# Gate and up products of two feed-forward blocks: token slices of 432, 424 and 424 instead of 256, 512 and 512

## The reference

```python
def swiglu(h, w_gate, w_up, w_down):
    return (jax.nn.silu(h @ w_gate) * (h @ w_up)) @ w_down

x = x + 0.5 * swiglu(rmsnorm(x, norm_ffn1[l]), w_ffn1_gate[l], w_ffn1_up[l], w_ffn1_down[l])
x = x + hybrid_mixer(rmsnorm(x, norm_mix[l]), w_in[l], ...)
x = x + 0.5 * swiglu(rmsnorm(x, norm_ffn2[l]), w_ffn2_gate[l], w_ffn2_up[l], w_ffn2_down[l])
```

## Time and profile before

| | |
|---|---|
| median of three runs | 2524.55 us |
| the profiled execution's own time | 2521.63 us |
| its span, first to last instruction | 2519.8 us |
| mean granted TensorE clock | 0.985 |
| TensorE matmul busy | 2437.7 us, 97% of the span |
| VectorE, ScalarE, GpSimd busy | 37%, 22%, 21% |

### The profile page before, as it was taken

How to read it: one execution, slowest core, us unless ns; L and a number is a source line. 1 busy time by engine, 2 the same in 40 slices (tenths; PEclk the granted TensorE clock), 3 DMA queues, 4 the chain that set the end, 5 groups by cost and what they waited for, 6 DMA issues and landing times. The chain is left out here.

```text
span 2519.8 us, 29661 instructions
## 1 busy us (share of the span) xinstructions
PE 2437.7 (97%) x12762; PEld 2037.1 (81%) x12762; DVE 923.0 (37%) x1453; ACT 555.3 (22%) x988; POOL 524.0 (21%) x283
## 2 busy tenths in 40 slices
PE   6999999999999999799998999999999999999998
PEld 5888888888888887666677878888888888888887
DVE  5322222132212246765636755622132212221224
ACT  4111111111111135533433221311111111111112
POOL 3121111111111123422213322111111111112111
PEclk8999999999999999899999999999999999999999
DMA  4110111111111125413234562011111111111012
GB/s 152 34 59 26 42 34 50 34 34 42 42 34 38 38 73 139 152 57 118 82 115 126 173 263 99 26 34 59 34 34 42 42 34 41 35 42 50 26 34 84
DMA packets 152003, 168.62 MB, mean 67 GB/s; under 512 B 15680, under 2 KB 124224, under 8 KB 151872
## 3 DMA queue, kind: packets, MB, share of 16 engines
q1 hardware_dynamic: 141504, 145.75, 18.7%
q10 hardware_dynamic: 10368, 20.98, 2.2%
HBM read 126.72 MB, written 36.70 MB: 65 GB/s over the span
## 5 line engine op out<-in xcount | busy, mean ns | idle before, releaser
L1320 PE MATMUL ps<-h_hi,w_hi 128*128 128x512 f32 (+2 forms) x2568 | 926.0, 361 | 14.4 <-ACT q_rot L806 5.8
L1321 PE MATMUL ps<-h_lo,w_hi 128*128 128x512 f32 (+2 forms) x2568 | 916.8, 357 | 0.0
L1322 PE MATMUL ps<-h_hi,w_lo 128*128 128x512 f32 (+2 forms) x2568 | 915.5, 356 | 0.0
L596 POOL TENSOR_TENSOR w_lo<-w_raw,w_hi 128x1024 fp32r<-128x1024 f32 x159 | 383.4, 2419 | 1773.6 <-ACT w_hi L721 1773.6
L1320 PEld LDWEIGHTS ps<-h_hi,w_hi 128*128 128x128 f32 (+1 forms) x2568 | 489.5, 191 | 105.5 <-issue 22.2
L1322 PEld LDWEIGHTS ps<-h_hi,w_lo 128*128 128x128 f32 (+1 forms) x2568 | 489.4, 191 | 70.5
L1321 PEld LDWEIGHTS ps<-h_lo,w_hi 128*128 128x128 f32 (+1 forms) x2568 | 490.0, 191 | 67.4
L1070 DVE TENSOR_TENSOR prod<-silu,ps 128x256 f32<-128x256 f32 x132 | 79.1, 599 | 983.0 <-PE ps L1322 978.1
L1360 PE MATMUL ps<-w_hi,hid_hi 128*128 128x512 f32 x880 | 343.0, 390 | 0.0
L1362 PE MATMUL ps<-w_hi,hid_lo 128*128 128x512 f32 x880 | 342.4, 389 | 0.0
L1361 PE MATMUL ps<-w_lo,hid_hi 128*128 128x512 f32 x880 | 342.3, 389 | 0.0
(11 more groups left out here) (131 smaller groups left out, 1495.6 us busy)
## 6 DMA issues: line engine op xcount, KB each, us to landing
w_raw<-in_w_ffn_gate SPq DMA_DIRECT2D x44, 512.0 KB, 3.8
w_raw<-in_w_ffn_up SPq DMA_DIRECT2D x44, 512.0 KB, 3.8
w_raw<-in_w_ffn_down SPq DMA_DIRECT2D x44, 512.0 KB, 3.5
w_raw<-in_w_in SPq DMA_DIRECT2D x14, 512.0 KB, 5.0
proj<-stage ACTq DMA_DIRECT2D x24, 256.0 KB, 2.1
x_mid<-x SPq DMA_DIRECT2D x10, 512.0 KB, 2.6
x<-in_x_sample SPq DMA_DIRECT2D x8, 512.0 KB, 8.2
proj<-gla_t ACTq DMA_DIRECT2D x4, 640.0 KB, 3.0
```

Of the source, the lines that this page charges most:

```text
L596: nc.gpsimd.tensor_tensor(w_lo[slot][:, :, :], w_raw[raw][:, :, :], w_hi[slot][:, :, :].bitcast(F32), ALU.subtract).then_inc(w_lo_ready, 1)
L1320: mm(out, hi, rhs_hi, start=first, stop=False)
L1321: mm(out, hi, rhs_lo, start=False, stop=False)
L1322: return mm(out, lo, rhs_hi, start=False, stop=last)
```

## The change

The old slices are kept for the first group of the first block. In all other groups (21 of 22) the slices are tokens 0 to 431, 432 to 855 and 856 to 1279. `prod` is computed with these widths, and the waits follow: for normalised tokens, the slice's end is rounded up to a whole tile; `ffn_down` waits for a slice's `hid_lo` at the tile in which the slice begins.

```diff
-SLICES = ((0, 256), (256, 512), (768, 512))
+FIRST_SLICES = ((0, 256), (256, 512), (768, 512))
+EVEN_SLICES = ((0, 432), (432, 424), (856, 424))
...
+def slices(early):
+    return FIRST_SLICES if early else EVEN_SLICES
...
# hidden on ScalarE, hidden on VectorE, and gate_up:
-                c0, n = SLICES[c]
+                c0, n = slices(A is A1 and i == 0)[c]
...
# gate_up
-                    pe.wait_ge(NORMS[n]["lo"], 2 * (c0 + m) // P)
+                    pe.wait_ge(NORMS[n]["lo"], 2 * ((c0 + m + P - 1) // P))
...
# ffn_down
-                for c, (c0, m) in enumerate(SLICES):
-                    if t * P == c0:
+                for c, (c0, m) in enumerate(slices(A is A1 and i == 0)):
+                    if t * P <= c0 < (t + 1) * P:
                         pe.wait_ge(A["hid_lo"], 6 * i + NCH + c + 1)
```

More of the change, by code:

```diff
@@ L1334, in gate_up @@
                 s = 6 * i + 3 * t + c
-                c0, m = SLICES[c]
+                c0, m = slices(A is A1 and i == 0)[c]
                 if s < NCH:
-                    pe.wait_ge(NORMS[n]["lo"], 2 * (c0 + m) // P)
+                    pe.wait_ge(NORMS[n]["lo"], 2 * ((c0 + m + P - 1) // P))
                 if c == 0:
```

## The result

The changed kernel takes 2530.34 us (median of 8 runs, 2527.72 to 2536.5) against 2524.23 us before (8 runs): ratio 1.0031, 95% interval 1.0021 to 1.0041. That is 5.3 to 10.3 us slower; the two medians differ by 6.1 us. In a second measurement (e3) the ratio was 1.0037 (1.0023 to 1.0050). The prediction was 2523.5 us and "the same"; the measured time lies inside the range, but the kernel is slower beyond the interval, so the likeliest case was wrong.

A forecast was written before the change was run, and what follows sets the result against it. TensorE's own matmul stream was taken as the bound. Matmuls 0, step between widths -0.8, ScalarE and VectorE -0.2, waits 0 gave -1.0 us: 2523.5 us on the median, "the same" (0.78), range 2517 to 2531.

The forecast's parts named there:

- What bounds the kernel: In the feed-forward groups TensorE waits for nothing; their length is the number of matmuls by the pitch of each.
- The matmuls of the changed slices: Gate and up of 21 groups: three pitches sum to 573.3 ns before and after, difference 0; bounds -80 and +215 us.
- The step between widths: The 0.02 us behind each 256-wide slice, 42 times in changed groups, was taken as gone: -0.8 us, bounds 0 and -1.7.
- ScalarE and VectorE: Their work follows the columns; only the narrower last slice at the first block's end counts: -0.2 us, bounds 0 and -0.3.
- the waits: Weight splits, raw-buffer loads, `prod` and `ffn_down` waits stay covered, with split slack falling from 6.1 to about 4.4 us: 0.
- the start of the second block: Slice 0 starts at the same place, the transposes about 3.5 us later, and later tiles stay hidden: 0.
- The misaligned third slice: Rival: rounded or misaligned columns, third slice starting at column 856 off 64 bytes, make the kernel slower; chance 0.10.
- the line: The pitch formula for a matmul of n columns at full clock: n/2.4 + 13.3 ns.
- half a block: A smaller case of the misaligned rival: half a block extra in the third slice alone, 6.7 us.
- Blocks of 16 columns: Case of the misaligned rival: TensorE handles whole blocks of 16, slices 1 and 2 cost 432 columns each: 13.4 us, 2537 us.
- The load-bound narrow slice: Rival: weight loads bind the 256-wide slice, the price per column is 0.443 ns: -13.4 us, 2511 us; chance 0.06.

The follow-up runs named there:

- e3: The changed kernel run again with no edit, against the kernel before: 2530.92 us, ratio 1.0037 (1.0023 to 1.0050).
- e2: The changed kernel with slices of 384, 448 and 448 columns, against the kernel before: 2551.29 us, ratio 1.0112 (1.0098 to 1.0127).
- e14: The changed kernel's width table set to (w, 512, 768 - w), w from 256 to 480: 512 columns cost 226.7 to 234.4 ns by start.
- e13: The changed kernel's table set to 21 triples around 300, 468, 512 and other orders: 468 columns cost 206.7 or 211.7 ns by start.
- e9: The 21 triples of a first width sweep, with 64 of 128 weight columns loaded in ten groups: 420-column slice 9.28 us before, 8.96 after.
- e7: The changed kernel's table set to other orders of widths, such as (448, 384, 448): 448 columns at token 0 cost 202.5 or 206.7 ns.

## Why the prediction was wrong, point by point

**What bounds the kernel: right.** TensorE's stream does, with no wait; this also holds after.

**The matmuls of the changed slices: the step that failed.** "The fixed part is equal at 256 and at 512, and I take it as equal between them." It is not equal between them: 15.9, 10.0 and 16.7 ns in the three new slices, and from 8.3 ns (268 columns at 0) to 22.4 (488 at 0) in the sweeps. The two widths of the trace happened to be multiples of 128 at starts that are multiples of 128, a family for which 13.3 ns held everywhere (120.0, 173.3, 226.7 ns). Two points on a line, both from a special family, said nothing of the widths between; my bounds (-80 and +215 us) admitted this, but the chance of 0.78 didn't. The term was forecast at 0 and is about +5.2 us: the three fixed parts are 42.6 ns together against 40.0, 2.6 ns x 2016. Gate and up of a group lasted 55.33 against 55.08 us, which says the same. The time stayed inside the range because the range made room for up to 3.5 ns a triple; the mechanism that was forecast, equal pitches for equal columns, is not what the runs show.

**The step between widths: wrong in sign.** I took -0.8 us; what is left of the 6.1 us is +0.9. Streams need a few matmuls to settle behind every change of pattern, also between 432 and 424 columns (the first distances of the second slice before are 234, 236, 228, 232 and 231 ns, then 227; after they are 195 and 191, then 187), so the steps inside gate and up cost as much as before (0.04 us a group). And behind the last slice the down products now take 27.25 instead of 27.20 us a group, 1.0 us in all.

**ScalarE and VectorE, the waits, the start of the second block: nothing against them.** VectorE's busy time is 922.6 us after and 923.0 before, no wait of TensorE appeared in either stretch of groups, and the second block starts with the same wait of 0.63 us. Gate and up of the second block's first group take 57.2 us against 57.0, no more than the 0.25 us of every other group, so there is no stall there. The -0.2 us at the end of the first block is too small to be seen, so it is neither confirmed nor refuted.

**The rivals.** The misaligned third slice was right that a start has a price: the slice that starts at 856 does cost 3.3 ns more than the line, 6.7 us, the price I had named for half a block. But the second gives 3.3 ns back and the first takes 2.6, so it is in part luck that the sum comes near that rival's. Blocks of 16 columns don't exist as a rule: e2 had only whole blocks and lost 28 us. The grid that a start has to meet is 64 columns for the 512-wide slice of e14, not 16. On this the Trainium skill's rule (SBUF — State Buffer, Door 1) of 16-byte lines spoke for no cost at all, since all starts of the change are whole lines; the runs differ from it, by 226.7 against 233.3 ns for 512 columns at starts 320 and 328, both whole lines, and the measurement decides. The load-bound narrow slice was wrong as put, since the price per column between narrow and wide isn't 0.443 ns. But something in it was right: 256 and 268 columns at token 0 cost the same 120.0 ns (e13), and with half the weights 256 columns cost 113.4 ns (e9), so 120 ns isn't simply 256 columns and a constant. The step of 0.02 us behind each narrow slice was a sign in the profile before that a stream carries something over from the one before it.

**Left open.** Measured is that the start in SBUF, the width and the work before have a part in the pitch, and that the output's place in its PSUM bank has none. That the weight load is the other party rests on e9 alone, whose edit also halves the partitions written. What the streams share, and so why a given width and start has its pitch, is not shown.

## What to carry to other kernels

Where the profile shows TensorE bound by its own stream, a change of width or start is a change of the pitch, and the pitch must be read from a trace at that very width and start, since a line through two round widths missed by up to 9 ns a matmul (488 columns at token 0 in e7: 225.7 ns, the line 216.7). Keep widths and starts of fp32r streams with a weight load each on multiples of 128 columns unless a sweep shows better; one kernel with a different table in each group measures some 40 to 60 pairs of width and start in one run. "More even" is no gain by itself when columns and instructions stay the same in number.

## What the runs showed of the hardware

At a granted clock of 1.00, a matmul of n fp32r columns with its own 128 by 128 weight load costs n/2.4 ns and a fixed part. That part is 13.3 ns for 256, 384 and 512 columns at multiples of 128, and 13.3 for 320 at 0. It is 10.0 for 424 at 432, and 20.0 for 448 at 384 in all groups of e2 but one. For 512 columns at a start off the grid of 64 it is 15.5 to 21. Starts a multiple of 128 columns apart gave the same: 424 columns at 344, 472 and 856 cost 193.3 to 193.4 ns. 256 and 268 columns at 0 cost the same 120.0 ns. A stream settles in a repeating pattern: at 432 columns from token 0, the distances of the starts repeat every eight matmuls (189, 192, 197, 198, 198, 202, 198, 193 ns), while the slice behind it has 187 ns throughout. One foreign matmul ahead of the slices of the change left their patterns as they were; a slice of another width changed that of 448 columns at 0, and 16 transposes that of 448 at 384. A weight load of 128 columns took 0.19 us in the trace, one of 64 columns 0.13. Two profiled executions of the changed kernel differed by 8.8 us in span with all pitches of the steady groups equal to 0.1 ns; 6.7 us of this lay in the mixer between the blocks, which took 685.7 to 696.3 us over the sixteen traces of this case.
